# Expert-row gathers written out one by one, without the GpSimd loop and its staging copies

## What is computed

```python
def peer_block(xb, w_q, key1, key2, u_tab, v_tab):
    q = (xb @ w_q)...reshape(T, 8, 2, 128)
    ...
    top, sel = lax.top_k(cand, 16)          # 16 experts for each of 8 heads
    eidx = jnp.take_along_axis(cidx, sel, axis=-1)
    gate = jax.nn.softmax(top, axis=-1)
    u = jnp.take(u_tab, eidx, axis=0)
    act = jax.nn.gelu(jnp.einsum('thkd,td->thk', u, xb))
    w = gate * act
    v = jnp.take(v_tab, eidx, axis=0)
    return jnp.einsum('thk,thkd->td', w, v)
```

## Time and profile before

| | |
|---|---|
| median of 3 runs | 5539.22 us (5529.06 to 5552.45) |
| span of the profiled execution | 5549.3 us; what lies around it isn't shown |
| PE, DVE, ACT, POOL busy | 68%, 43%, 12%, 44% of the span |
| mean granted TensorE clock | 0.845 |
| POOL's DMA queue | 309,312 packets, 1126.31 MB, 56.9% of 16 DMA engines' span |
| gathers, copies of row numbers | 2,080 and 256 |

### The profile page before, as it was taken

How to read it: one execution, slowest core, us unless ns; L and a number is a source line. 1 busy time by engine, 2 the same in 40 slices (tenths; PEclk the granted TensorE clock), 3 DMA queues, 4 the chain that set the end, 5 groups by cost and what they waited for, 6 DMA issues and landing times.

```text
span 5549.3 us, 41085 instructions
## 1 busy us (share of the span) xinstructions
PE 3779.2 (68%) x9698; PEld 1553.9 (28%) x9698; DVE 2408.2 (43%) x5178; ACT 691.5 (12%) x1601; POOL 2468.2 (44%) x2425
## 2 busy tenths in 40 slices
PE   8899998978028647647658847983066476386388
PEld 1243333334013222212223324441032132132133
DVE  3123223222774483483470263115764563654640
ACT  1110000110001111111111121010011011021011
POOL 0001001000677777777765100003767767767754
PEclk9898898979569979979979965996589789799799
DMA  7712212120789989989988342013889999999987
GB/s 235 236 60 89 85 61 94 64 77 31 273 308 331 347 315 342 346 301 344 340 319 331 124 66 92 31 54 116 304 311 348 340 326 334 342 324 346 334 306 251
DMA packets 413616, 1287.12 MB, mean 232 GB/s; under 512 B 59636, under 2 KB 83348, under 8 KB 412509
## 3 DMA queue, kind: packets, MB, share of 16 engines
q0 software_dynamic: 309312, 1126.31, 56.9%
q1 hardware_dynamic: 95716, 157.07, 9.0%
q10 hardware_dynamic: 8500, 2.70, 0.2%
HBM read 1257.15 MB, written 28.79 MB: 232 GB/s over the span
## 4 chain that ended last, share of the span: by engine, by line
PE 45%; issue 21%; POOL 16%; DMA 11%; DVE 5%; POOLq 1%; ACT 1%; ACTq 0%; SPq 0%; DVEq 0%; another core or an unknown queue 0%
PE ps L1551 17%; POOL w L1119 9%; PE ps L1405 7%; POOL arena L1119 6%; DMA arena<-in_peer_v_dram,arena 4%; PE ps L1520 4%; PE ps L1376 3%; PE ps L1485 2%; PE ps L653 2%; DMA w<-in_peer_u_dram,arena 2%; DMA arena<-in_state_ret_dram 2%; PE ps L566 1%; PE ps L634 1%; POOL arena L1140 1%; DMA w<-in_w_ada_dram 1%
## 5 line engine op out<-in xcount | busy, mean ns | idle before, releaser
L1551 PE MATMUL ps<-arena 128*128 128x512 f32 x4096 | 1952.0, 624 | 1445.6 <-issue 584.2
L1831 DVE CUSTOM_DVE_ANT_0 w<-w,h 128x1024 f32<-128x1024 f32 x1024 | 1255.3, 1227 | 1225.4 <-DMA w<-in_peer_u_dram,arena 1190.4
L1551 PEld LDWEIGHTS ps<-arena 128*128 128x128 f32 x4096 | 767.0, 196 | 2629.2 <-issue 2014.0
L1119 POOL DMA_INDIRECT w<-in_peer_u_dram,arena x1040 | 1181.7, 1136 | 430.8 <-issue 277.7
L1119 POOL DMA_INDIRECT arena<-in_peer_v_dram,arena x1040 | 1116.6, 1074 | 514.7 <-issue 257.1
L1316 ACT ACTIVATE arena<-ident,arena 128x128 f32<-128x128 f32 x1024 | 409.7, 403 | 1941.4 <-PE ps L1551 1537.4
L1405 PE MATMUL ps<-w,hT 128*128 128x512 f32 (+1 forms) x960 | 415.7, 593 | 3.3 <-DVE arena L1729 2.9
L1063 POOL TENSOR_TENSOR rstd<-var,mhalf 128x5 f32<-128x5 f32 x5 | 6.0, 1190 | 883.1 <-DVE var L1596 883.1
L1140 POOL COPY arena<-arena 128x8 uint32 x256 | 107.0, 418 | 422.8 <-DVE arena L1794 399.7
L1079 POOL TENSOR_TENSOR rstd<-var,mhalf 128x4 f32<-128x4 f32 x4 | 4.1, 1027 | 625.3 <-DVE var L1694 625.3
L1520 PE MATMUL ps<-hT,w 128*128 128x512 f32 x512 | 275.2, 629 | 0.0
(11 more groups left out here) (289 smaller groups left out, 2926.8 us busy)
## 6 DMA issues: line engine op xcount, KB each, us to landing
w<-in_w_ada_dram SPq DMA_DIRECT2D x48, 1024.0 KB, 7.2
w<-in_ret_w_in_dram SPq DMA_DIRECT2D x24, 1024.0 KB, 7.3
out_dram<-arena POOLq DMA_DIRECT2D x36, 512.0 KB, 3.3
w<-in_peer_u_dram,arena POOLq DMA_INDIRECT x1040
arena<-in_peer_v_dram,arena POOLq DMA_INDIRECT x1040
arena<-in_state_ret_dram POOLq DMA_DIRECT2D x32, 512.0 KB, 4.8
w<-in_peer_w_q_dram SPq DMA_DIRECT2D x16, 1024.0 KB, 7.3
w<-in_ret_w_out_dram SPq DMA_DIRECT2D x8, 1024.0 KB, 5.9
```

What stands on the lines that cost most here:

```text
L1119: pool.indirect_dma_start(ring[:, slot, :], None, table, bass.IndirectOffsetOnAxis(ap=index, axis=0)).then_inc(landed_sem[slot], 16)
L1551: mm = pe.matmul(ps[:, bank + half, :], diag[:, s % 4], v_ring[:, s % RING, half * BW:(half + 1) * BW], start=False, stop=False)
L1831: dve.tensor_tensor_reduce(u_ring[:, s % RING], u_ring[:, s % RING], h[:, t], 1.0, 0.0, ALU.mult, ALU.add, dots[:, s:s + 1]).then_inc(u_us ...
```

## The change

The loop on POOL is replaced by straight code: each gather is written out with a wait on a constant, and its row number is read directly from `eidx`. The copies, their staging buffers, the semaphore for them and the increments of `issued` are gone. The order of the gathers and the condition for each slot stay as they were. Nothing changes on the other engines.

```diff
--- before.py
+++ after.py
@@ -211,8 +211,6 @@
         gate = cut(TILES, NE)
         eidx_s = cut(NS, dtype=U32)
         gate_s = cut(NS)
-        stage_u = cut(2, RING, dtype=U32)
-        stage_v = cut(2, RING, dtype=U32)
         wgt_s = cut(NS * NS)
 
         cut = Cut(hT[:, :, :].rearrange("p c n -> p (c n)"))
@@ -262,7 +260,7 @@
         gelu_in, gelu_tanh, wgt_done, diag_done = sem("gelu_in"), sem("gelu_tanh"), sem("wgt_done"), sem("diag_done")
         mix_ps, wz_zero = sem("mix_ps"), sem("wz_zero")
         out_st = sem("out_st")
-        steps_v, steps_p = sem("steps_v"), sem("steps_p")
+        steps_v = sem("steps_v")
 
         def slot_free(n):
             return n + BATCH - RING + 1
@@ -442,7 +440,7 @@
             sp.dma_start(h[:, 0:TP, :], z_d[0:PROMPT].rearrange("(t p) n -> p t n", p=P)).then_inc(z_ld, 16)
             sp.dma_start(h[0:NS, TP, :], z_d[PROMPT:NTOK]).then_inc(z_ld, 16)
 
-        def ssm_pool(pool, link, root):
+        def ssm_pool(pool, root):
             root(SSM_ROOT)
 
         def sines(act):
@@ -1048,7 +1046,6 @@
 
         @block.gpsimd
         def _(pool):
-            link = Steps(pool, steps_p)
             pool.memset(ident[:, :], 0.0).then_inc(consts, 1)
             pool.memset(zeros[:, :], 0.0).then_inc(consts, 1)
             pool.memset(mhalf[:, :], -0.5).then_inc(consts, 1)
@@ -1123,34 +1120,18 @@
                 root(PEER_ROOT[layer])
                 ut = peer_u.rearrange("l e n -> (l e) n")
                 vt = peer_v.rearrange("l e n -> (l e) n")
-                u_lane = (u_ring, ut, stage_u, u_used, u_ld)
-                v_lane = (v_ring, vt, stage_v, v_used, v_ld)
+                u_lane = (u_ring, ut, u_used, u_ld)
+                v_lane = (v_ring, vt, v_used, v_ld)
 
                 def gathers(count, lanes):
-
-
-                    with pool.Fori(0, count // BATCH) as i:
-                        link.loop(i, 2 * len(lanes))
-                        for half in range(2):
-                            for (ring, table, stage, used, ld), tile, first in lanes:
-                                n = gather_of(layer, tile) + first + half * RING
-
-                                pool.wait_ge(used, i * BATCH + (n + BATCH - RING))
-                                pool.sem_inc(issued, 1)
-                                link.link(pool.tensor_copy(stage[:, half],
-                                                           eidx[:, tile, bass.ds(i * BATCH + (first + half * RING), RING)]))
-                                pool.sem_inc(issued, 1)
-                            for s in range(RING):
-                                for (ring, table, stage, used, ld), tile, first in lanes:
-                                    n = gather_of(layer, tile) + first + half * RING + s
-                                    pool.wait_ge(used, i * BATCH + slot_free(n))
-                                    pool.sem_inc(issued, 1)
-                                    gather(ring, s, table, stage[:, half, s:s + 1], ld)
-                    link.end(count // BATCH)
+                    for k in range(count):
+                        for (ring, table, used, ld), tile, first in lanes:
+                            pool.wait_ge(used, slot_free(gather_of(layer, tile) + first + k))
+                            gather(ring, (first + k) % RING, table, eidx[:, tile, first + k:first + k + 1], ld)
 
                 def sample_gathers(lane_):
 
-                    ring, table, _, used, ld = lane_
+                    ring, table, used, ld = lane_
                     for b in range(NS):
                         pool.wait_ge(used, slot_free(gather_of(layer, TP) + b))
                         gather(ring, b, table, eidx_s[:, b:b + 1], ld)
@@ -1170,7 +1151,7 @@
                 sample_gathers(v_lane)
 
             peer(0)
-            ssm_pool(pool, link, root)
+            ssm_pool(pool, root)
             peer(1)
             root(NORMS)
```

## The result

The changed kernel takes 5240.18 us (median of 4 runs, 5226.13 to 5247.71) against 5534.14 us before: a ratio of 0.9462, 95% interval 0.9439 to 0.9486, 294 us less. I had forecast 92 us less, with a range that ended at 5390.

The account below looks back on a forecast made before the run. POOL's successive gathers were taken to bound u first, pairs and u alone, DMA close behind; 24 + 44 + 24 = 92 us saved took the span of 5549.3 to 5457, median forecast 5447 us, range 5390 to 5525.

Parts of the forecast that it names:

- u first: Stage of 128 u gathers and 16 copies, 215 to 223 us, set by POOL; forecast saving 12 us, twice: 24.
- pairs: Stages of 80 u and 80 v gathers and 20 copies, about 241 us, set by POOL; forecast 7.4 us, six times: 44.
- u alone: Stages of 48 u gathers and 6 copies, about 78 us, set by POOL; forecast 4 us, six times: 24.
- v alone: Stages of 48 v gathers, paced by PE at 1.72 us a gather; forecast saving nothing.
- the layer's end: Last stages of a layer's expert mixer, where PE sets the rate; forecast saving nothing.
- term of 44 us: Six pairs stages: DMA share rises from 0.95 to an assumed 0.98, saving 7.4 us each.
- I take the lower: POOL's saving, bounded by 146 and 202 us: 146 chosen, with all the copies' waiting passed to gathers.
- fixed, as forecast: On POOL's path: 188 copies' minimum time 38 us, 128 blocks' gaps 86, gaps between paired copies about 22: 146 us.
- none handed on: Upper bound of POOL's saving, 202 us: none of the copies' 56 us of waiting returns on gathers.
- POOL and the dots fall into step: Slower rival: DVE's dots hold u gathers throughout, up to 5657 us; chance 0.10, shared with slow fetching of straight code.
- The loop's cost, "nothing": POOL's loop waits, register arithmetic and `issued` increments are hidden behind the running gather; subtracting them saves nothing.

Follow-up runs that it names:

- e4: Changed kernel with DVE's dot products replaced by sums that read one SBUF operand (product left out): 5117 us, ratio 0.9226 to the kernel before.
- e2: Changed kernel with the copies made again, but gathers neither read them nor wait for them: 5380 us, ratio 0.9691 to the kernel before.
- e9: Changed kernel plus a write-only POOL memset of 512 columns before every eighth gather of a block: 5405 us, ratio 0.9769 to the kernel before.
- e11: Changed kernel with the waited-for copies back and one-operand sums instead of dot products: 5132 us, ratio 0.9266 to the kernel before.
- e8: Changed kernel with the waited-for copies and the `issued` increments back, waits still constants: 5507 us, ratio 0.9942 to the kernel before.
- e7: Changed kernel plus a write-only POOL memset of 8 numbers a partition before every eighth gather: 5248 us, ratio 0.9452 to the kernel before.

## Why the prediction was wrong

The direction, the place and the stages were right. Three steps stood: POOL sets the rate in u first, pairs and u alone; a written-out gather costs what a looped one does, 0.94 and 0.30 us; v alone and the layer's end give nothing. Straight code was fetched without a stall: in the pairs stages the idle before a gather stayed 0.30 us. That POOL would then wait for slots there was wrong; it didn't. The sum failed in two places.

1. **"DMA share is 0.94 and 0.96 ... I take 0.98: 241 x (1 - 0.95/0.98) = 7.4 us".** This term of 44 us measured 205. I read the share as a part of a fixed capacity: 344 GB/s at 0.94 would end at 366. After the change the same gathers run at 407 GB/s and 1.02, and e4 shows 400 to 410 as the end. So per busy time the engines had moved 8% less (366 against 399) than they can; why, no run shows. The rule of the Trainium skill that I had set beside it (DMA: Bandwidth & Descriptors, "Where 436 GB/s comes from", near 358 GB/s for one core's reads from HBM) gave an estimate of 8 us. The page works that figure out as half of what two cores share; here one core ran and moved 407, and the measurement decides. The row that didn't fit it, 381 GB/s in 15 us, was the better sign, and I passed over it.

2. **"A removed copy may hand its wait to the next gather ... I take the lower".** In fact the gathers' own waits shrank. I had bounded the change at POOL by 146 to 202 us, and on POOL's path it was about 146 (fixed, as forecast) + 50 (the copies' waiting) + 113 (the gathers' waiting) = 309, of 312 measured. In one pairs stage: 14.4 us of fixed copy time, 1 to 6 of copies' waiting, and 160 x (1.09 - 0.973) = 19 of gathers' waiting make 37, as measured (241 to 204). My bound "none handed on" left out that it can go the other way. I had drawn it from two stages, with 4.7 us less on copies and 3.7 more on gathers, too small a difference to carry a rule. This step weighs more than the first: with all the DMA room there is, my sum would have ended at 146 to 202 us less, not at 294.

The rival "POOL and the dots fall into step" named the mechanism with the wrong sign. They do fall into step when nothing disturbs them, but in five of six stages into one in which the dot starts just behind the v gather's start, and almost no gather is held over 0.1 us. What broke it was the copy block, every eight pairs. e2, e9 and e11 show that: unlinked copies cost 140 us, a pause of pure writing 165, and linked copies 6.5 us a pairs stage once the DVE instruction holds nobody. Why this step attracts and the other mostly doesn't stays open; with u gathers landing 6.6 us after issue (median), each dot's start follows an earlier gather's, so POOL's delays come back to it through the dots, but I didn't vary the latency.

The loop's cost, "nothing", holds between gathers only. Behind a linked copy the sequencer's work is uncovered, as I had said of the cover, but I had put the whole 0.97 us down to the copy: about 66 us of the kernel's time come from the `issued` increments (e8), some 38 from the rest of the loop.

u first and u alone, 24 + 24 forecast, gave 54 + 53. The second reason is small there, as their gathers' waiting shrank by 8 and 7 us only. Most of it is fixed time (28 and 31) and the copies' waiting (13 and 13), which I had counted as handed on or cut off at the DMA room.

## What to carry to other kernels

Where one engine's instructions hold another's, and the first in turn waits for what the second brings, a small instruction costs its length and what it does to the phase of the two: count how often the held instruction is caught, and look at what a steady pattern of the two would be. A removal can then give back more than everything that is removed. A DMA share just under 1.0 isn't a ceiling; take the best GB/s of any window with the same kind of packets as the least that is possible. Increments and register work of POOL's sequencer cost nothing while a gather was running (0.30 us of idle with and without them), and 0.37 to 0.44 us behind a copy that was waited for.

## What the runs showed of the hardware beyond that

Gathers of 128 rows of 4 KB reached 405 to 407 GB/s on one core over 200 us, and 410 over 66 us in e4. A gather is held only at its start: gathers that began 0.2 us ahead of a dot took 0.94 us, those held by one that was already running ended about 0.80 us after it (dot over at 1906.80, gather over at 1907.60). The holding goes one way: none of the dots, neither before nor after, took over 1.32 us. A POOL memset of 0.12 us between two gathers is free (e7).
